# Residual sums and norms of a two-block transformer moved from feature rows to token rows

## The reference

```
h = rms_norm(x, g_pre) * (1 + scale) + shift
x = x + w * (1 + gate) * rms_norm(y, g_post)      # w is 0.5, 1 or 0.5
```

```
h = rmsnorm(x, g);  x = x + mixer(h)
h = rmsnorm(x, g);  x = x + (silu(h @ w1) * (h @ w3)) @ w2
```

## Time and profile before

| | us |
|---|---|
| median of 3 runs | 2637.39 |
| the profiled execution | 2633.77 |
| its span | 2632.2 |
| PE busy (its weight loads) | 2444.6 (2198.4) |
| DVE busy | 1649.7 |
| ACT busy | 1213.5 |
| mean granted TensorE clock (1 is full) | 0.953 |

### The profile page before, as it was taken

How to read it: one execution, slowest core, us unless ns; L and a number is a source line. 1 busy time by engine, 2 the same in 40 slices (tenths; PEclk the granted TensorE clock), 3 DMA queues, 4 the chain that set the end, 5 groups by cost and what they waited for, 6 DMA issues and landing times.

```text
span 2632.2 us, 43807 instructions
## 1 busy us (share of the span) xinstructions
PE 2444.6 (93%) x16456; PEld 2198.4 (84%) x16456; DVE 1649.7 (63%) x2386; ACT 1213.5 (46%) x1574; POOL 73.2 (3%) x141
## 2 busy tenths in 40 slices
PE   3998998989989999998989988999999889999998
PEld 2997987879979988877979987699899886898997
DVE  6877666656768776666565554455655555455655
ACT  3444456444445444554344454355544444364443
POOL 0100000000000000000000000000000000000000
PEclk8999999999999999989999998899999988899999
DMA  7875554436656774544435533144455441244452
GB/s 305 283 282 185 192 184 156 158 128 224 252 179 246 281 256 144 185 152 161 160 129 186 180 128 128 53 153 160 172 183 191 145 145 65 98 157 163 176 183 104
DMA packets 74142, 461.53 MB, mean 175 GB/s; under 512 B 8272, under 2 KB 8416, under 8 KB 27648
## 3 DMA queue, kind: packets, MB, share of 16 engines
q1 hardware_dynamic: 53424, 384.33, 40.6%
q0 software_dynamic: 19120, 70.43, 7.6%
q10 hardware_dynamic: 1440, 4.62, 0.5%
HBM read 458.30 MB, written 1.05 MB: 175 GB/s over the span
## 4 chain that ended last, share of the span: by engine, by line
PE 85%; ACT 5%; DVE 4%; issue 4%; DMA 1%; DVEq 1%; ACTq 0%; SPq 0%
PE ps L628 19%; PE ps L374 15%; PE ps L375 15%; PE ps L376 15%; PE ps L630 10%; ACT whi L971 2%; PE ps L507 1%; PE ps L458 1%; PE ps L435 1%; PE ps L474 1%; DMA set_a<-in_ada 1%; PE ps L487 1%; PE ps L473 1%; DVE wlo L1414 1%; PE ps L508 1%
## 5 line engine op out<-in xcount | busy, mean ns | idle before, releaser
L1414 DVE TENSOR_TENSOR wlo<-raw,whi 128x2048 fp32r<-128x2048 f32 x360 | 824.2, 2291 | 282.0 <-ACT whi L971 263.1
L971 ACT ACTIVATE whi<-raw 128x2048 fp32r<-128x2048 f32 x360 | 687.5, 1910 | 245.4 <-PE ps L376 239.5
L628 PE MATMUL ps<-hx,whi 128*128 128x512 f32 x2112 | 755.9, 401 | 34.2 <-DVE hx L1484 29.2
L630 PE MATMUL ps<-hx,wlo 128*128 128x256 f32 x2112 | 596.0, 282 | 0.0
L628 PEld LDWEIGHTS ps<-hx,whi 128*128 128x128 f32 x2112 | 400.3, 190 | 134.0 <-DVE hx L1484 31.2
L374 PE MATMUL ps<-hx,whi 128*128 128x256 f32 x1680 | 498.1, 297 | 12.6 <-DVE hx L1482 7.3
L375 PE MATMUL ps<-hx,whi 128*128 128x256 f32 x1680 | 482.5, 287 | 0.0
L376 PE MATMUL ps<-hx,wlo 128*128 128x256 f32 x1680 | 482.0, 287 | 0.0
L374 PE MATMUL ps<-yhi,whi 128*128 128x256 f32 x1440 | 410.8, 285 | 0.0
L375 PE MATMUL ps<-ylo,whi 128*128 128x256 f32 x1440 | 408.1, 283 | 0.0
L376 PE MATMUL ps<-yhi,wlo 128*128 128x256 f32 x1440 | 407.8, 283 | 0.0
(11 more groups left out here) (250 smaller groups left out, 2588.5 us busy)
## 6 DMA issues: line engine op xcount, KB each, us to landing
raw<-in_w SPq DMA_DIRECT2D x360, 1024.0 KB, 4.8
adat<-in_ada POOLq DMA_DIRECT2D x128, 512.0 KB, 4.5
raw<-in_ada SPq DMA_DIRECT2D x4, 512.0 KB, 11.5
blk<-in_block POOLq DMA_DIRECT2D x2, 990.5 KB, 5.0
set_a<-in_ada SPq DMA_DIRECT2D x3, 512.0 KB, 25.2
raw<-in_ada ACTq DMA_DIRECT2D x2, 512.0 KB, 12.0
set_b<-in_ada ACTq DMA_DIRECT2D x2, 512.0 KB, 17.6
x<-in_x SPq DMA_DIRECT2D x1, 1024.0 KB, 18.9
```

Source lines behind the costliest of these rows:

```text
L628: mm(ps[:, bank + i, :].rearrange("p (a s) -> p a s", a=2), whi[:, slot, col:col + P], hx[:, :, k, :], start=(k == 0), stop=False)
L630: last = mm(ps[:, bank + i, 0:S], wlo[:, slot, col:col + P], hhi[:, k, :], start=False, stop=(k == KD - 1))
L971: A(whi[:, slot, :], raw[:, slot, :], ACT.Copy).then_inc(*T.counts("hi_ready"))
L1414: tt(wlo[:, slot, :], raw[:, slot, :], whi[:, slot, :].bitcast(F32), ALU.subtract)\
```

## The change

x, the results and the residual sums are now held by token: [128 tokens, 2 halves, 1024 features]. A down tile and an output-projection tile have the activations as the stationary operand and 512 weight columns as the moving one; PSUM bank 2t + c holds token half t and column half c. The output projection's tiles are cut otherwise: lower or upper half of the inner features by 512 columns, so each is used once. The FFN's tile order is changed at the end: the last three down tiles follow each other after the last up tile.

Norms: ACT squares 512 columns and accumulates them over the free dimension (`accum_out`), and the root is three activations of one column (`row_root`). The gate (with the post-norm's gain) has to lie along columns: PE transposes its broadcast columns (`gate_row`) before the last tile, and ACT copies it to `g_row`. DVE multiplies the result by it, adds it to x with the root as a per-partition scalar, and scales x to unit rows (`unit_rows`). PE transposes these to PSUM (`turn_rows`), and ACT and DVE, four blocks each, apply gain and shift and make the two parts of h.

The seam is cut in token halves: an FFN's last tile finishes the two banks of half 0 before those of half 1 (the output projection's half 0 is full after the first part of its last tile), and the first two tiles of the next sublayer are each done for half 0, then for half 1 (`first_tiles`), with 128 tokens to a matmul. All other tiles take all 256 tokens at once, as before. The output is written in two transfers, one for each token half. `N_LOADS`, semaphore counts and the layouts of x, the final norm's gain and the output follow. Of the diff, the core and the new functions:

```diff
+            def turn_rows(t):
+                for b in range(2):
+                    pe.wait_ge(*T.next("u_ready"))
+                    for m in range(4):
+                        c0 = (4 * b + m) * P
+                        last = nc.tensor.transpose(ps[:, (0 if t else 6) + b, m * P:(m + 1) * P],
+                                                   unit_x[:, t, c0:c0 + P], ident)
+                    last.then_inc(*T.counts("tr_ready"))
+            def gate_row(i):
+                pe.wait_ge(*T.next("gcol_ready"))
+                for m in range(KD):
+                    last = nc.tensor.transpose(ps[:, 4 + m // 4, m % 4 * P:(m % 4 + 1) * P],
+                                               modf[:, i, 16 + m:17 + m].broadcast_to([P, P]), ident)
+                last.then_inc(*T.counts("grow_out"))
+            def half_tokens(t, group, new):
+                for k in range(KD):
+                    if new and k % 2 == 0:
+                        pe.wait_ge(*T.next("h_ready"))
+                    for i in range(2):
+                        last = group(i, k, slice(t * P, (t + 1) * P))
+                return last
+            def first_tiles(opens):
+                first = opens(0, tile())
+                half_tokens(0, first, True)
+                turn_rows(1)
+                second = opens(1, tile())
+                half_tokens(0, second, False)
+                half_tokens(1, first, True).then_inc(*T.counts("tile_used"))
+                half_tokens(1, second, False).then_inc(*T.counts("tile_used"))
...
-            def output_projection():
-                def part(i, slot, half):
-                    for j in range(2):
-                        last = blocks(acc[:, 2 * i + j, :],
-                                      [(whi[:, slot, k * 256 + j * P:k * 256 + (j + 1) * P],
-                                        wlo[:, slot, k * 256 + j * P:k * 256 + (j + 1) * P],
-                                        hhi[:, k, :], hlo[:, k, :]) for k in range(4 * half, 4 * half + 4)],
-                                      start=(half == 0 and j == 0), stop=(half == 1), skip=True)
-                    return last
+            def output_projection(gate=None):
+                def rows(slot, lower, c, t):
+                    return blocks(ps[:, 2 * t + c, :],
+                                  [(hhi[:, 4 * lower + k, t * P:(t + 1) * P], hlo[:, 4 * lower + k, t * P:(t + 1) * P],
+                                    whi[:, slot, k * 512:(k + 1) * 512], wlo[:, slot, k * 512:(k + 1) * 512])
+                                   for k in range(4)], start=(lower == 0), stop=(lower == 1))
                 pe.wait_ge(*T.next("ml_ready"))
-                slots = []
+                for c_ in range(2):
+                    slot = tile()
+                    rows(slot, 0, c_, 0)
+                    rows(slot, 0, c_, 1).then_inc(*T.counts("tile_used"))
+                pe.wait_ge(*T.next("ml_ready"))
+                pe.wait_ge(*T.nth("pj_out", T.n["fills"]))
+                wait_bank6()
+                if gate is not None:
+                    gate_row(gate)
+                for c_ in range(2):
+                    slot = tile()
+                    rows(slot, 1, c_, 0).then_inc(*T.counts("bank_done"))
+                    rows(slot, 1, c_, 1).then_inc(*T.counts("tile_used"))
+                turn_rows(0)
...
+            def wide(bank, slot, col, k, at):
+                out = ps[:, bank, :].rearrange("p (a s) -> p a s", a=2)
+                mm(out[:, :, at], whi[:, slot, col:col + P], hx[:, :, k, at],
+                   start=(k == 0 and at.start == 0), stop=False, skip_group_check=True)
+                return mm(out[:, 0, at], wlo[:, slot, col:col + P], hhi[:, k, at],
+                          start=False, stop=(k == KD - 1), skip_group_check=True)
+            def first_gate_up():
+                T.n["g_chunks"] += 1
+                def opens(n, slot):
+                    return lambda i, k, at: wide((4, 6)[n] + i, slot, k * 256 + i * P, k, at)
+                first_tiles(opens)
...
+            def down_rows(slot, place, c, t, first=False, end=False):
+                a, o = place
+                return blocks(ps[:, 2 * t + c, :],
+                              [(yhi[:, a, o + cc, t * P:(t + 1) * P], ylo[:, a, o + cc, t * P:(t + 1) * P],
+                                whi[:, slot, cc * D + c * 512:cc * D + (c + 1) * 512],
+                                wlo[:, slot, cc * D + c * 512:cc * D + (c + 1) * 512]) for cc in range(2)],
+                              start=first, stop=end, skip=True)
+            def down(parity, first=False):
+                for b in range(4):
+                    last = down_rows(slot, (parity, 0), b % 2, b // 2, first)
+            def ffn(gate=None):
+                first_gate_up()
+                with T.loop((NJ - 5) // 2, FFN_BODY):
+                gate_up()
+                gate_up()
+                down(0)
+                down(1)
+                slot = tile()
+                pe.wait_ge(*T.next("a_ready"))
+                if gate is not None:
+                    gate_row(gate)
+                for c_ in range(2):
+                    down_rows(slot, (0, 2), c_, 0, end=True).then_inc(*T.counts("bank_done"))
+                down_rows(slot, (0, 2), 0, 1, end=True).then_inc(*T.counts("bank_done"))
+                down_rows(slot, (0, 2), 1, 1, end=True).then_inc(*T.counts("tile_used"))
+                turn_rows(0)
...
+            def row_root(t, dst, ready):
+                act.drain()
+                A(part[:, t:t + 1], sums[:, t, 0:1], ACT.Identity, bias=c("eps"), scale=1.0 / D)
+                act.drain()
+                A(part[:, t:t + 1], sums[:, t, 1:2], ACT.Ln, bias=part[:, t:t + 1], scale=1.0 / D)
+                act.drain()
+                A(dst[:, t:t + 1], part[:, t:t + 1], ACT.Exp, scale=-0.5).then_inc(*ready)
+            def x_root(t):
+                for c_ in range(2):
+                    act.wait_ge(*T.next("x_ready"))
+                    A(res[:, t, 512 * c_:512 * c_ + 512], x[:, t, 512 * c_:512 * c_ + 512], ACT.Square,
+                      accum_out=sums[:, t, c_:c_ + 1])
+                row_root(t, r_x, T.counts("x_rms"))
+            def result_root(t, dones, ready):
+                for c_ in range(2):
+                    act.wait_ge(*T.next(dones[c_]))
+                    A(res[:, t, 512 * c_:512 * c_ + 512], ps[:, 2 * t + c_, :], ACT.Square,
+                      accum_out=sums[:, t, c_:c_ + 1]).then_inc(*T.counts("bsq_ready"))
+                row_root(t, r_res, T.counts(ready))
+            def result_kept(dones):
+                for c_ in range(2):
+                    act.wait_ge(*T.next(dones[c_]))
+                    A(res[:, 1, 512 * c_:512 * c_ + 512], ps[:, 2 + c_, :], ACT.Copy)
+                A(r_res[:, 1:2], c("inv1024")[:, 0:1], ACT.Copy, scale=float(D)).then_inc(*T.counts("gb_rms"))
+            def sublayer_end(plain, more, lasts):
+                if not plain:
+                    act.wait_ge(*T.next("grow_out"))
+                    A(g_row, ps[:, 4:6, :].rearrange("p b s -> p (b s)"), ACT.Copy).then_inc(*T.counts("grow_ready"))
+                if more is None:
+                    split_ahead()
...
+                if plain:
+                    T.n["bank_done"] += 2
+                else:
+                    result_root(0, ("bank_done", "bank_done"), "ga_rms")
+                x_root(0)
+                T.n["tile_used"] += 2 - lasts.count("tile_used")
+                if plain:
+                    result_kept(lasts)
+                else:
+                    result_root(1, lasts, "gb_rms")
+            def high_parts(t, gain, shift):
+                bank, at = (0 if t else 6), slice(t * P, (t + 1) * P)
+                act.wait_ge(*T.next("tr_ready"))
+                for m in range(4):
+                    src = ps[:, bank, m * P:(m + 1) * P]
...
+                        A(h32[:, m, at], src, ACT.Identity, scale=gain[:, m:m + 1], bias=shift[:, m:m + 1])
+                    if m % 2:
+                        act.drain()
+                        A(hhi[:, m - 1:m + 1, at], h32[:, m - 1:m + 1, at], ACT.Copy).then_inc(*T.counts("hh_ready"))
+                T.n["tr_ready"] += 1
+                for m in (4, 6):
+                    A(hhi[:, m:m + 2, at], h32[:, m:m + 2, at], ACT.Copy).then_inc(*T.counts("hh_ready"))
+            def sublayer_begin(gain, shift=None, new_gain=True):
+                if new_gain:
+                    act.wait_ge(*T.next("mods_ready"))
+                high_parts(0, gain, shift)
+                x_root(1)
+                split_high()
+                high_parts(1, gain, shift)
...
+            def gated(t):
+                for c_ in range(2):
+                    v.wait_ge(*T.next("bsq_ready"))
+                    at = slice(512 * c_, 512 * c_ + 512)
+                    tt(res[:, t, at], ps[:, 2 * t + c_, :], g_row[:, at], ALU.mult)
+                v.drain()
```

(59 more changed lines are left out.)

422 lines of the change are left out of this document (152 added, 270 removed).

## The result

The changed kernel takes 2698.5 us, median of 4 runs (2687.32 to 2713.42), where the kernel before takes 2633.36 (2624.84 to 2640.12, 4 runs): a ratio of 1.0259, 95% interval 1.0231 to 1.0287. The forecast was 2667 in a range of 2610 to 2730. The direction was right, the size was not: +65 us where +30 was said. The profiled executions are 2690.16 against 2633.77, spans 2688.5 against 2632.2 (+56.4); the other 9 us are executions of the changed kernel that are longer than the profiled one.

The account below looks back on a forecast made before the run. TensorE's own work plus its standstills was taken as the bound. Cheaper tiles, means and gate rows (-17.8, -5.5), seams (+27, +4.5, -6, +10.6, +10.3), start +10 and end -1 gave +32 us: 2667, range 2610 to 2730.

Parts of the forecast that it names:

- 512-column tiles: Down and plain output-projection tiles: 24 matmuls of 512 columns for 48 of 256, 5.52 for 5.76 us; 74 tiles, -17.8 us.
- means and gate rows: Last FFN tiles: six means go, -9 us; four transposed gate rows come, +3.5; together -5.5 us.
- The price at full clock: First two tiles of each stage: a 128-column matmul can't beat its weight load, 0.115 us each, 5.5 per projection half tile.
- B: Half tiles: the load is hidden and a 128-column matmul costs half, 0.06 us; 2619 us in all; chance 0.10.
- B': Half tiles: loads partly hidden, 0.08 us a matmul; 2637 us, no change; chance 0.07.
- C: Half tiles: a short fp32r matmul loses the fast rate and costs 0.22 us like fp32; 2762 us; chance 0.10.
- The chain: Seams: first product 8.4 us after a normed FFN's last tile, where it was 14.3; plain output projection's first h at 2.5.
- Rival D: Seams: token half 1 is not late, PE never waits after its first half tile; 45 us less, 2622; chance 0.13.
- Rival E: Normed output projection: the new tile order fails and the stall stays, +12 us; chance 0.60 shared with the main case.
- The clock of the half tiles: Seams: half tiles priced at full clock; the wait for half 1 hides the first one's low clock.
- the forecast wait: Seams: after its first half tile PE waits for half 1's unit rows, going on at 18.8 us behind a normed FFN.
- Nothing waits for them: DMAs: same tiles, sizes and queue, two of a sublayer some us later, one small POOL broadcast; no engine waits, no cost.

Follow-up runs that it names:

- rows first: Changed kernel with VectorE making token half 1's unit rows before the second tile's low split, not after it: 2691.5 us, ratio 1.0206.
- second profile: The changed kernel run once more without any edit: 2699.84 us, span 2698.2.

## Why the prediction was right or wrong

Right, with their sizes:
- 512-column tiles: 0.23 us a matmul, 5.45 a tile; with means and gate rows -23.6 for -21.3. The output projection's stall is gone, -6.7 twice for -6.5.
- The price at full clock: a 128-column fp32r matmul starts every 0.112 us (said 0.115), nearly the 0.12 of one of 256 columns, as the forecast's bound by the load would have it; rivals B (0.06), B' (0.08) and C (0.22) fall. The Trainium skill's 81 ns (TensorE: Matmul & The Clock Gate, Back-to-back issue gap) is not met here: the measurement is 112. A pair of 256 and 128 columns takes 0.23, as said, though its parts divide as 0.17 and 0.06, not 0.12 and 0.115.
- The chain: first product at 8.5 us for 8.4 after a normed FFN, 6.3 for 6.2 after a normed projection, 2.8 for 2.5 after a plain one.
- Rival D (half 1 not late): late it is; making it earlier moved the median by 7 us, not by 45; with whole tiles an earlier half 1 was worth 51. Rival E: the stall did not stay.

Wrong:
- **The clock of the half tiles is the step that failed.** The working priced every half tile behind the wait at full clock (5.5 us, with 1 or 1.7 us a seam added for the clock) and let the wait for half 1 hide the first one's low clock. At the projections a half tile at 1.2 GHz takes 10.3 us. Behind the first two normed FFNs it fills the stretch to 18.85 us by itself, so that the forecast wait isn't there, and the number 18.8 was met for another reason. At two seams it sets the end: at the passage between the stacks (12.3 + 10.3 = 22.6 where 18.8 was said, +3.7 us) and behind the plain FFN (16.8 where 12.9 + 2.6 was said, +1.3). These are 5.0 of the seams' 12.7 us in the profile; the rest, up to 2.4 us a seam, was not taken apart. Another 15 us come each time that a stream of 144 half matmuls stays low to its end, as in one seam of the second profile. The four runs, 2687, 2690, 2707 and 2713, are spread as none and one or two such seams would spread them, and their mean granted clocks fall in the same order (0.942, 0.940, 0.935, 0.933); which runs had them is not known.
- "Nothing waits for them" was wrong for one transfer. At the passage between the stacks h is there 9.4 us after the last tile, and the first product starts 2.9 us after that, behind the block of constants. The transfer is asked for 7.0 us after the tile and takes 5.0 to land, so once h came earlier the transfer was the later of the two, and the low half tile behind it carries most of the delay to the end of the seam (9.4 + 10.3 = 19.7 without it, 22.6 with it).
- The working took it that PE leaves the low clock once it has work without gaps. The rows of before could not show otherwise: they have no narrow stream. The Trainium skill's rule that activity releases the throttle (TensorE: Matmul & The Clock Gate, What's actually happening) would say the same; in the windows above PE has no gap for 30 to 40 us and the clock stays at 0.50 (0.52 where it was full for the first 2 us), so for a 128-column fp32r stream the measurement decides against it.
- The attention sections were put at 0, with no range for their clock: +13.4 in this profile, the largest single miss in it, and up to 20 between executions. How much of it the change causes stays open.
- A slip in the sum: the four output tiles, 4 x 5.52 + 0.9 + 0.8, are 23.8 and not 24.1; the trace has 24.1.
- The halves were judged right in sign only: they cost 38 us against whole tiles in the same order (rows first), and stand in the way of an order that gives 51 more.

Of the 65 us, the profile accounts for 56.4: forecast 32, seams 12.7, attention 13.4, the start and the end 2.5, less 4.5 in FFNs and output tiles. The rest is the executions' spread. Open stays what in a narrow stream keeps the clock down, and why the same program gets out of it in one execution and not in another.

## What to carry to other kernels

Before cutting a tile into token halves to start earlier, price the halves at both clocks and count how many stand on the path: with fp32r operands and a fresh load for each, 128 columns cost as much as 256 at full clock (0.112 and 0.12 us here), and about twice that where such matmuls alone follow each other and the clock is low (0.214). Interleave wider matmuls, or do the tile whole and shorten the chain ahead of it. When a chain gets shorter, look at what else its end waits for: a transfer that used to land in time may be the new end. A wait that can't be removed may be filled with matmuls into a free bank, if their time is measured first; here it paid with 256 and 512 columns behind it (19 us) and not with 128.

## What the runs showed of the hardware

- An unbroken stream of 128-column fp32r matmuls, each behind its load, never raised the granted clock from 0.5: 30.4 us with PE busy 30.40. It also fell from 1.00 to 0.5 about 2 us into such a stream. With 256 columns at the same count it was 1.00 (23.6 us for 39.6). Twice the columns were 16 us faster in one seam and 78 over the kernel (ratios 1.0269 and 1.0591, each beside its own runs of the kernel before).
- It is no fixed outcome: with eight fp32 transposes in the middle the same program went on at full clock in one execution and stayed low in another, 50.6 us for 35.4 in one seam.
- A filling fp32 matmul of 256 columns takes 0.44 us (40 passes in 8.79 us).
- Sections of unchanged code varied by 20 us in 1155 with the granted clock, 0.35 us for each us at half clock.
